# Output-projection units placed between the attention steps of the last head pair of a hybrid decoder block

## What is computed

```python
h = rms_norm(x, g_in)
qA, kA, vA, qB, kB, vB, qM, gate, qI, kI, wI = split(h @ w_in)
kM, vM = split(rms_norm(mem, g_mem) @ w_mem_kv)
o = concatenate([dilated(qA, kA, vA), dsa(qB, kB, vB, qI, kI, wI), memory(qM, kM, vM)])
o = o * silu(gate)
return rms_norm(x + o @ w_out, g_final)
```

## Time and profile before

| | us |
|---|---|
| median of 3 runs (770.96 to 774.82) | 773.7 |
| the profiled execution | 768.31 |
| its span, first to last instruction | 766.5 |
| PE busy | 697.1 (91%) |
| DVE busy | 435.5 (57%) |
| ACT busy | 334.3 (44%) |
| POOL busy | 131.7 (17%) |
| mean granted TensorE clock | 0.982 of full speed |

### The profile page before, as it was taken

One profiled execution on the slowest core, in us unless ns is written; L12 is line 12 of the kernel. 1 busy time (PEld: TensorE's weight loads), 2 busy tenths in 40 slices (PEclk: granted clock), 3 DMA queues, 4 the chain that ended last, 5 costly groups with the idle time before them and its releaser, 6 DMA issues. The chain is left out here.

```text
span 766.5 us, 11469 instructions
## 1 busy us (share of the span) xinstructions
PE 697.1 (91%) x4229; PEld 546.3 (71%) x4229; DVE 435.5 (57%) x1012; ACT 334.3 (44%) x633; POOL 131.7 (17%) x94
## 2 busy tenths in 40 slices
PE   2889999898999999899989998999979967899996
PEld 2668888666777777677767776777767655678884
DVE  4765775267464586647664786479733445322433
...
DMA packets 53175, 48.76 MB, mean 64 GB/s; under 512 B 5744, under 2 KB 45696, under 8 KB 53120
## 3 DMA queue, kind: packets, MB, share of 16 engines
...
...
## 5 line engine op out<-in xcount | busy, mean ns | idle before, releaser
L1250 PE MATMUL j_ps<-h_hi,w_hl 128*128 128x512 f32 (+1 forms) x624 | 208.8, 398 | 0.9 <-issue 0.9
L1250 PEld LDWEIGHTS j_ps<-h_hi,w_hl 128*128 128x128 f32 (+1 forms) x624 | 115.7, 185 | 26.0 <-issue 1.5
L572 POOL TENSOR_TENSOR w_hl<-w_raw,w_hl 128x1024 fp32r<-128x1024 f32 (+1 forms) x30 | 70.8, 2360 | 360.8 <-ACT w_hl L665 360.8
L1250 PE MATMUL j_ps<-h_lo,w_hl 128*128 128x512 f32 (+1 forms) x312 | 121.7, 390 | 0.0
L817 ACT ACTIVATE prob<-prob,nmax 128x256 f32<-128x256 f32 (+7 forms) x128 | 89.7, 702 | 51.2 <-DVE nmax L1094 42.8
L805 ACT ACTIVATE probT<-pt_ps 128x512 f32<-128x512 f32 (+3 forms) x88 | 41.4, 470 | 131.7 <-PE pt_ps L1361 131.0
L1250 PE MATMUL s_ps<-h_hi,w_hl 128*128 128x512 f32 x240 | 79.0, 398 | 0.4 <-POOL w_hl L572 0.4
L1361 PE MATMUL pt_ps<-ident,prob 128*128 128x128 f32 x496 | 75.1, 286 | 4.5 <-DVE gate L1121 3.8
L1361 PEld LDWEIGHTS pt_ps<-ident,prob 128*128 128x128 f32 x496 | 54.1, 143 | 25.2 <-issue 21.2
L1020 DVE TENSOR_SCALAR_CACHE_REDUCE picked<-idx,tk 128x384 f32<-128x384 f32 (+5 forms) x72 | 67.8, 942 | 1.4
L1250 PEld LDWEIGHTS j_ps<-h_lo,w_hl 128*128 128x128 f32 (+1 forms) x312 | 58.1, 186 | 11.0
...
## 6 DMA issues: line engine op xcount, KB each, us to landing
w_raw<-in_w_in_dram SPq DMA_DIRECT2D x28, 512.0 KB, 3.8
bias<-in_a_tab_dram SPq DMA_DIRECT2D x8, 512.0 KB, 4.7
...
bias<-in_w_out_dram SPq DMA_DIRECT2D x6, 512.0 KB, 3.8
idx<-in_x_dram SPq DMA_DIRECT2D x4, 512.0 KB, 5.2
probT<-in_w_mem_kv_dram SPq DMA_DIRECT2D x4, 512.0 KB, 6.6
prob<-in_x_dram SPq DMA_DIRECT2D x4, 512.0 KB, 4.4
```

The lines of the kernel that those rows point to most:

```text
L572: pool.tensor_tensor(w_hl[:, w % 2, 1, :, 0:n], w_raw[:, :, 0:n], w_hl[:, w % 2, 0, :, 0:n].bitcast(F32), ALU.subtract).then_inc(w_lo_read ...
L1250: last = pe.matmul(bank[0:n, :], a[:, k, 0:n], c[:, k, HALF * b:HALF * b + HALF], start=(k == 0 and q == 0), stop=(k == KD - 1 and q == 2))
```

## The change

Input projections end with pair 6's gate: the last q moves from steps 54 and 55 to steps 48 and 49, and goes to its own place in `qk` (`Q_SLOT`), since pair 6 still reads its own q. Steps 52 to 55 then carry no fill. The splits of `w_out` move from steps 56 to 59 to steps 52 to 55, two tiles in each; the rooms of `w_out` are now half of `v_sb`, `picked` and `w_raw`. Pairs 6 and 7 no longer go through DRAM: `part_hi` on ACT and `part_lo` on POOL split 512 tokens of them at once into free places of `qk` (steps 53, 56, 60, 64), and the loads and splits of the other six pairs are 128x768 instead of 128x896. Sixteen units are placed in steps 56 to 64 (`FILL_OUT`), in the order of tiles 4, 5, 6, 7, 0, 1, 2, 3. The eight of tiles 4 to 7 leave out the last pair (21 matmuls); its product for them is made behind everything, 6 matmuls for each tile (`project_last`), and added by `add_last`. So the number of matmuls is the same. Rows 0 to 3 are scaled on ACT (`scale_row`) and multiplied with `g_final` on POOL, rows 4 to 7 on DVE as before. `gf_row` has a place of its own.

```diff
+        if p == NP - 2:
+            out += [q_tile(p + 1)]
...
-        if follows:
+        if follows and p < NP - 2:
             out += [q_tile(p + 1)]
...
+Q_SLOT = [0] * (NP - 1) + [2]
...
+        if (what, p) == ("q", NP - 2):
+            at = 0
...
-WO_PER_STEP = [3, 2, 2, 1]
+WO_PER_STEP = [2, 2, 2, 2]
+WO_FIRST = STEPS - NT - len(WO_PER_STEP)
 WO_ROOMS = 3
-EARLY = NT // 2
-
-
-EARLY_OUT = {STEPS - 3: (None, (0, 0), None), STEPS - 2: ((0, 1), (1, 0), None),
-             STEPS - 1: ((1, 1), (2, 0), None), STEPS: ((2, 1), (3, 0), (3, 1))}
+
+OUT_TILES = [4, 5, 6, 7, 0, 1, 2, 3]
+OUT_UNITS = [(t, b) for t in OUT_TILES for b in range(2)]
+LATE = [4, 5, 6, 7]
+
+FILL_OUT = {STEPS - 8: (None, None, (4, 0)),
+            STEPS - 7: ((4, 1), None, (5, 0)),
+            STEPS - 6: ((5, 1), None, (6, 0)),
+            STEPS - 5: ((6, 1), None, (7, 0)),
+            STEPS - 4: ((7, 1), None, (0, 0)),
+            STEPS - 3: ((0, 1), (1, 0), None),
+            STEPS - 2: ((1, 1), (2, 0), None),
+            STEPS - 1: ((2, 1), None, None),
+            STEPS: ((3, 0), None, (3, 1))}
+LENT_OUT = [(4, 0), (5, 0), (6, 0)]
+
+MIX_AT = {STEPS - NT - 3: [0], STEPS - NT - 2: [1], STEPS - 7: [2], STEPS - 6: [3],
+          STEPS - 5: [4], STEPS - 4: [5], STEPS - 3: [6], STEPS - 2: [7]}
+
+PART_AT = {STEPS - NT - 3: (NP - 2, 0), STEPS - NT: (NP - 2, 1), STEPS - 4: (NP - 1, 0), STEPS: (NP - 1, 1)}
+PARTS = list(PART_AT.values())
+PART_SLOT = {NP - 2: 6, NP - 1: 4}
+
...
+        gf_row = sb("gf_row", [P, D])
...
         wo_hi, wo_lo = h_hi, h_lo
-        wo_raw = [bias[:, 0, :], bias[:, 1, :], w_raw[:, :, :].rearrange("p k m -> p (k m)")]
-
-        y_rows = [gate[:, :], v_sb[:, 1, :, :].rearrange("p t f -> p (t f)"), dist[:, :], picked[:, :],
-                  prob[:, 0, 0, :], prob[:, 1, 0, :], prob[:, 0, 1, :], prob[:, 1, 1, :]]
-        gf_row = idx[:, 0:T]
-        sq_junk = qk[:, 2, :]
-
-        mixed = [bias[:, b, 0:(NP - 1) * P].rearrange("p (q t) -> p q t", q=NP - 1) for b in range(2)]
+        wo_raw = [v_sb[:, 1, :, :].rearrange("p t f -> p (t f)"), picked[:, :],
+                  w_raw[:, :, :].rearrange("p k m -> p (k m)")]
+        y_rows = [gate[:, :], idx[:, 0:T], idx[:, T:2 * T], idx[:, 2 * T:3 * T], *wo_raw, dist[:, :]]
+        sq_junk = qk[:, 0, :]
+        mixed = [bias[:, b, 0:(NP - 2) * P].rearrange("p (q t) -> p q t", q=NP - 2) for b in range(2)]
...
+        def out_bank(t, b):
+            return s_ps[0][:, HALF:T] if (t, b) in LENT_OUT else j_ps[:, :]
...
             def load_wo(n):
-                if n == WO_ROOMS - 1:
+                if n == 0:
+                    sp.wait_ge(pv_done, CHUNK0[STEPS - 2 * NT])
+                if n == 1:
+                    sp.wait_ge(mask_ready, len(IDX_TILES))
+                if n == 2:
                     sp.wait_ge(w_hi_ready, N_W)
                     sp.wait_ge(w_lo_ready, N_W)
                 if n >= WO_ROOMS:
...
+                if at == 1:
                     load_wo(0)
                     load_wo(1)
-                if last >= 0:
-
-                    for n in wo_of_step(s):
-                        if WO_ROOMS <= n + WO_ROOMS - 1 < NP:
-                            load_wo(n + WO_ROOMS - 1)
-                if last == 4:
+                if at == 2:
+                    load_wo(2)
+                    load_mixed(0)
+                    load_mixed(1)
+                for n in wo_of_step(s):
+                    if n + WO_ROOMS < NP:
+                        load_wo(n + WO_ROOMS)
+                if at == NT - 1:
+                    sp.dma_start(gf_row[:, :], g_final.unsqueeze(0).broadcast_to([P, D])).then_inc(gf_in, 16)
                     for b in range(2):
                         sp.wait_ge(wo_lo_ready[b], NP // 2)
-                        load_mixed(b)
-                    for g in range(2):
-                        sp.wait_ge(og_stored[g], 16 * (NP - 1))
+                    for t in LATE[:WO_ROOMS]:
+                        load_residual(t)
+                if at == NT + 1:
+                    load_mixed(2)
+                    for a in range(2):
+                        sp.wait_ge(biased[a], STEPS - NT + FIRST_TOPK)
+                    load_residual(7)
+                    sp.wait_ge(part_lo_ready, 2)
                     load_residual(0)
-                    sp.wait_ge(pv_done, CHUNK0[STEPS - 2 * NT])
-                    load_residual(1)
+                    load_mixed(3)
+                if NT + 2 <= at < NT + 6:
+                    load_mixed(at - NT + 2)
+                if at >= NT + 5:
                     for a in range(2):
                         sp.wait_ge(biased[a], s)
-                    load_residual(2)
...
-                last_lo(t)
+                for n in MIX_AT.get(s, []):
+                    mix_lo(n)
+                if s in PART_AT:
+                    part_lo(s)
+
+            part_lo(STEPS)
+            pool.wait_ge(gf_in, 16)
+            for t in range(4):
+                pool.wait_ge(y_scaled, t + 1)
+                pool.tensor_tensor(y_rows[t], y_rows[t], gf_row[:, :], ALU.mult).then_inc(y_final_pool, 1)
...
+            def part_hi(s):
+
+                p, g = PART_AT[s]
+                tokens = slice(HALF * g, HALF * g + HALF)
+                act.wait_ge(og_ready, 2 * p + g + 1)
+                act.activation(qk[:, PART_SLOT[p], tokens], gates(p)[:, tokens], ACT.Copy).then_inc(part_hi_ready, 1)
+
...
+                for n in MIX_AT.get(s, []):
+                    mix_hi(n)
+                if s in PART_AT:
+                    part_hi(s)
+                if STEPS - 2 <= s < STEPS:
+                    square_row(s - STEPS + 2)
             assert m == len(uses)
...
-                    last_hi(ahead)
-                square_row(t)
-                if t >= EARLY - 1:
-                    y_root(t - EARLY + 1, 0 if t < EARLY else t, t + 1)
+            square_row(2)
+            square_row(3)
+            y_root(0, 0, 4)
+
+            def scale_row(t):
+                act.activation(y_rows[t], y_rows[t], ACT.Copy, scale=stat[:, 3, t:t + 1]).then_inc(y_scaled, 1)
+
+            act.wait_ge(y_inverse, 1)
+            scale_row(0)
+            scale_row(1)
+            square_row(4)
+            y_root(1, 4, 5)
+            scale_row(2)
+            square_row(5)
+            y_root(2, 5, 6)
+            scale_row(3)
+            square_row(6)
+            y_root(3, 6, 7)
+            square_row(7)
+            y_root(4, 7, 8)
...
+            def add_last(n):
+
+                row = y_rows[LATE[n]]
+                dve.wait_ge(out_done, len(OUT_UNITS) + n + 1)
+                dve.wait_ge(y_added, unit_number(LATE[n], 1) + 1)
+                dve.tensor_tensor(row, s_ps[n % 2][:, :], row, ALU.add).then_inc(last_added, 1)
...
+            start_norm(0, 0, 4)
+            dve.drain().then_inc(y_inverse, 1)
+            add_last(1)
+            add_last(2)
             dve.wait_ge(gf_in, 16)
-            final_norm(0, 0, EARLY)
-            for t in range(EARLY, NT):
-                add_residual(t, 0)
-                add_residual(t, 1)
-                final_norm(t - EARLY + 1, t, t + 1)
+            start_norm(1, 4, 5)
+            final_norm(4)
+            add_last(3)
+            for n in range(1, 4):
+                start_norm(n + 1, LATE[n], LATE[n] + 1)
...
-                elif t < EARLY + 2:
-                    pe.wait_ge(biased[t % 2], STEPS)
+                    for a in range(2):
+                        pe.wait_ge(biased[a], STEPS - NT)
+                if unit_before(t, b):
+                    pe.wait_ge(y_added, unit_before(t, b))
                 else:
-                    pe.wait_ge(y_added, 2 * (t - 2) + b + 1)
+                    wait_evacuated(pe, len(uses) - 1)
                 if b == 0:
-                    pe.wait_ge(mix_lo_ready, t + 1)
-                    pe.wait_ge(last_lo_ready, t + 1)
-                hi, lo = w_hl[:, t % 2, 0], w_hl[:, t % 2, 1]
+                    pe.wait_ge(mix_lo_ready, n + 1)
+                hi, lo = w_hl[:, n % 2, 0], w_hl[:, n % 2, 1]
                 passes = [(hi, wo_hi), (hi, wo_lo), (lo, wo_hi)]
-                cut = slice(HALF * b, HALF * b + HALF)
-                bank = j_ps[:, :] if t < EARLY else s_ps[t % 2][:, cut]
-                for p in range(NP):
+                for p in range(NP - 2):
                     for q, (a, c) in enumerate(passes):
-                        last = pe.matmul(bank, a[:, p, :], c[:, p, cut],
-                                         start=(p == 0 and q == 0), stop=(p == NP - 1 and q == 2))
+                        pe.matmul(bank, a[:, p, :], c[:, p, cut], start=(p == 0 and q == 0), stop=False)
+                pairs = [NP - 2] + ([] if t in LATE else [NP - 1])
+                for p in pairs:
+                    pe.wait_ge(part_lo_ready, PARTS.index((p, t // 4)) + 1)
+                    for q, (a, c) in enumerate(parts_of(p, t, b)):
```

(47 more changed lines are left out.)

168 lines of the change are left out of this document (78 added, 90 removed).

## The result

The changed kernel takes 788.4 us (median; 786.2 to 789.2), beside 772.4 us for the kernel before on the same chip: a ratio of 1.019, 95% interval 1.015 to 1.023. The forecast was 787.5 against 773.7, which is 1.018. The profiled execution has a span of 784.4 us, 17.9 us more than before.

A forecast was written before the change was run, and what follows sets the result against it. PE's chain of waits bounds the kernel; only idle time, clock and end can change. Gone 26.7 us, new 25.9 in the middle and 9.6 + 5 at the end: +13.8, 787.5 us against the median; range 770 to 795.

The forecast's parts named there:

- The total: Whole kernel: +13.8 us, 782.1 against the profiled 768.3, and 787.5 against the median 773.7; forecast chance 0.66.
- Steps 48 and 49: Two fills cover 4.05 us of idle time but for 0.4: -3.6 us, and -1.3 for the clock drop behind.
- Steps 52 to 55: Without cover and with the splits, rounds of 9.4 to 9.9 us; PE idles 17.0 us, between 8 and 24.
- step 56: Begins 35.0 us behind step 52 with a low part unfinished; PE waits 3.2 and 0.9, 4.1 us in all.
- the waits: Sign of being right: four PE waits of 3 to 5 us from step 52, released by a `probT` copy.
- The clock: Lower granted clock after PE's long waits in step 53 and the next: 3 us, between 0 and 6.
- gaps later: Steps 63 and 64: two places with nothing between a copy and its values, 0.9 us each, 1.8 in all.
- The end: From the end of unit (3, 1): 22.7 us instead of 13.1, +9.6, at least +8.1, before POOL's delay.
- POOL's part: At the end, POOL's four multiplications hold up DVE's small two-input instructions: +5 us, between 0 and 8.
- No exclusion: Second rival: beside POOL, DVE's low parts take 1.23 us and small instructions 0.16; +3.8, 777.5 us; chance 0.13.
- The splits hide: First rival: splits fit existing gaps in steps 52 to 55, PE loses 2 us a step; -7.3, 766.4 us; chance 0.14.
- Late rows: Third rival: tile 4 or 5's row loads come late, DVE holds the next biases; +22, 795.5 us; chance 0.07.

## Why the prediction was right, point by point

- **The total.** +13.8 us forecast; from step 48 on the profiled executions show +14.45, the medians +16.0, the ratio 1.019 instead of 1.018.
- **Steps 48 and 49.** 0.4 us idle, as said.
- **Steps 52 to 55.** The round was right: DVE through with the first low part 10.3 us behind step 52 (605.55 - 595.28), values at 12.7 where I had 12.9. The values of steps 54 and 55 followed at 9.96 and 9.41 us (rounds of 9.4 to 9.9 forecast). The size was split wrongly. I had 17.0 us of idle time and 3.0 for the clock; step 56 came 36.9 us behind step 52, not 35.0. Nor did the waits look as announced: not four of 3 to 5 us but 5.16, 1.76, 3.85 and 2.59 in steps 53 to 56, each in front of the values and ended by DVE's copy of `probT` (for the first the profile names no releaser; the copy ended at 607.90).
- **The clock** is the term that was mis-sized. Busy time times missing share, over the five stretches below 1.00 ahead of the end, is 1.3 + 1.8 + 1.0 + 0.9 + 1.9 = 6.9 us, beyond the bound of 6. Idle time was less by as much: 13.9 and 3.1 (step 56) instead of 17.0 and 4.1, since slow matmuls fill the same waits. With 2.0 of gaps later (I had 1.8), the middle sums to 25.9, the figure of the forecast. That the sum is exact is luck in its parts.
- **The end.** 22.4 us without POOL's part, where I had 22.7; POOL's part 5.5 where I had 5. The root began 1.30 us behind the start of its table load (758.36, 759.66), and in front of the load ACT stood still for 0.02 us. The Trainium skill (ScalarE: Activation LUTs, What ACT_TABLE_LOAD costs) gives 2.66 us for load and drain together, which would have made the end 24.1; the trace shows no drain.
- **No exclusion** (second rival) is refuted by two runs, each taking POOL's work away: 2.55 to 1.22 us, and 2.06 to 0.16. By the Trainium skill (SBUF — State Buffer, Who interferes with whom) a DVE instruction with two SBUF inputs contends with a GpSimd instruction that reads SBUF, under an exclusive lock, and the order of issue decides who blocks; these rows agree, and the 1.23 us of POOL's eight columns show the other direction. Its price was more than the forecast's: 7.8 and 5.2 us by the runs, where 5.0 and 5 stood.
- **The splits hide** (first rival): PE idled 17.0 us from step 52 to the first unit, above its 15 but not by much, and 5.0 us of slow matmuls came on top. The same rival describes the kernel with the low part one step later (8.9 us idle in steps 52 to 55, where the rival had 8): there they do hide. What decided was a place in DVE's order, as the forecast argued.
- **Late rows** (third rival): DVE's additions waited for PE alone, and PE idled 2.0 us in 116 us of units.
- **Where the reasoning was wrong.** "The timeline tells why steps 56 to 61 are slow: a low part of `w_out` sits on DVE in front of the next step's biases" took one wait for the cause. Moving that low part gained nothing there, since the landing of the `w_out` tiles held ACT, and PE behind it, to the same time. The number was not hurt, since it took the idle time as it stood in the rows.
- **Not foreseen** were the 3.45 us before step 48, which belong to the execution.
